# Expert gate/up tiles of 4 depth blocks by 1024 columns, activations transposed on VectorE, down rows in pairs

## What is computed

```python
def moe_ffn(u, router_w, w_gate_up, w_down):
    ...
    for e in range(N_EXPERTS):
        y = y + dense_gates[:, e:e + 1].astype(tok.dtype) * swiglu(tok, w_gate_up[e], w_down[e])
...
def swiglu(u, w_gate_up, w_down):
    g, up = jnp.split(u @ w_gate_up, 2, axis=-1)
    return (jax.nn.silu(g) * up) @ w_down
```

## Time and profile before

| | us |
|---|---|
| median of three runs | 1164.14 |
| span of the profiled execution | 1161.9 |
| first expert product in it | 423.45 |
| one job in it | 90.82 |
| TensorE busy | 1147.7 |
| VectorE busy | 289.3 |
| ScalarE busy | 284.7 |

### The profile page before, as it was taken

How to read it: one execution, slowest core, us unless ns; L and a number is a source line. 1 busy time by engine, 2 the same in 40 slices (tenths; PEclk the granted TensorE clock), 3 DMA queues, 4 the chain that set the end, 5 groups by cost and what they waited for, 6 DMA issues and landing times.

```text
span 1161.9 us, 31779 instructions
## 1 busy us (share of the span) xinstructions
PE 1147.7 (99%) x14480; PEld 1010.9 (87%) x14480; DVE 289.3 (25%) x474; ACT 284.7 (25%) x480; POOL 30.7 (3%) x84
## 2 busy tenths in 40 slices
PE   8999999999999999999999999999999999999997
PEld 7768999999998888888888888888888898988885
DVE  3776654554653430000000000000000000000002
ACT  4766543443548430011001011001001001001001
POOL 0000000000000011000000000000000000000100
PEclk9999999999999999999999999999999999999999
DMA  9649965552254399989999999999999999999993
GB/s 339 221 131 289 359 218 192 197 186 89 101 190 146 106 391 389 351 322 383 377 393 395 367 394 395 359 392 395 383 379 396 395 359 394 394 368 393 391 379 137
DMA packets 174368, 361.21 MB, mean 311 GB/s; under 512 B 6616, under 2 KB 50048, under 8 KB 174240
## 3 DMA queue, kind: packets, MB, share of 16 engines
q1 hardware_dynamic: 169936, 343.78, 80.7%
q0 software_dynamic: 4080, 15.34, 4.0%
q10 hardware_dynamic: 224, 0.09, 0.0%
HBM read 347.65 MB, written 11.53 MB: 309 GB/s over the span
## 4 chain that ended last, share of the span: by engine, by line
PE 92%; DMA 3%; DVE 2%; ACT 1%; SPq 1%; issue 0%; ACTq 0%; DVEq 0%
PE pair L962 57%; PE pair L531 9%; PE pair L532 9%; PE pair L533 9%; DMA dn_ring<-in_moe_w_down 3%; PE pair L1005 2%; PE pair L567 1%; PE pair L593 1%; SPq L462 1%; DMA norm_rows<-in_b_norm_w 0%; PE pair L944 0%; DVE up_lo L1626 0%; PE pair L632 0%; DVE dn_ring L1731 0%; PE pair L934 0%
## 5 line engine op out<-in xcount | busy, mean ns | idle before, releaser
L962 PE MATMUL pair<-up_ring,work 128*32 128x384 f32 (+1 forms) x6144 | 358.0, 380 | 0.0
L962 PEld LDWEIGHTS pair<-up_ring,work 128*32 128x32 f32 x6144 | 343.0, 110 | 9.5 <-issue 4.0
L962 PE MATMUL pair<-dn_ring,kT_a 128*32 128x256 f32 (+1 forms) x3168 | 250.5, 450 | 3.0 <-DMA dn_ring<-in_moe_w_down 2.1
L962 PEld LDWEIGHTS pair<-dn_ring,kT_a 128*32 128x32 f32 x3168 | 163.1, 110 | 61.5 <-DMA dn_ring<-in_moe_w_down 3.0
L2022 DVE TENSOR_TENSOR work<-work,pair 128x384 f32<-128x384 f32 x40 | 22.2, 554 | 507.0 <-PE pair L962 507.0
L1118 ACT ACTIVATE kT_a<-pair 128x384 f32<-128x384 f32 (+3 forms) x65 | 25.3, 401 | 488.6 <-PE pair L1005 488.5
L531 PE MATMUL pair<-uT_hi,up_hi 128*128 128x256 f32 x480 | 135.5, 282 | 0.8 <-DVE uT_lo L1640 0.6
L962 PE MATMUL pair<-up_more,work 128*32 128x384 f32 (+1 forms) x2304 | 136.0, 380 | 0.0
L532 PE MATMUL pair<-uT_lo,up_hi 128*128 128x256 f32 x480 | 134.8, 281 | 0.0
L533 PE MATMUL pair<-uT_hi,up_lo 128*128 128x256 f32 x480 | 134.8, 281 | 0.0
L1626 DVE TENSOR_TENSOR up_lo<-up_ring,up_hi 128x2048 fp32r<-128x2048 f32 x46 | 105.3, 2291 | 112.9 <-ACT up_hi L1118 112.8
(11 more groups left out here) (304 smaller groups left out, 794.8 us busy)
## 6 DMA issues: line engine op xcount, KB each, us to landing
up_ring<-in_moe_w_gate_up SPq DMA_DIRECT2D x128, 1024.0 KB, 13.0
dn_ring<-in_moe_w_down SPq DMA_DIRECT2D x88, 1024.0 KB, 15.1
up_more<-in_moe_w_gate_up SPq DMA_DIRECT2D x48, 1024.0 KB, 14.5
up_ring<-in_dense_w_gate_up SPq DMA_DIRECT2D x22, 1024.0 KB, 9.3
dn_ring<-in_dense_w_down SPq DMA_DIRECT2D x11, 1024.0 KB, 11.3
up_ring<-in_kv_w SPq DMA_DIRECT2D x4, 2048.0 KB, 8.1
y_rows<-q_T POOLq DMA_DIRECT2D x1, 6528.0 KB, 33.5
up_ring<-in_a_w_in SPq DMA_DIRECT2D x4, 1024.0 KB, 12.7
```

The costliest lines, as they stand in the source:

```text
L962: return pe.matmul(out, a, w, start=start, stop=stop, tile_position=(0, THIRD * place), skip_group_check=True)
```

## The change

- Gate and up tiles are 4 depth blocks by 1024 columns (768 in the last group). Four tiles make a group: gate with depth blocks 0 to 3 and 4 to 7, then up with the same. There are three groups, twelve tiles (E_UP). A row of a transfer is 4 KB (3 KB in the last group).
- In each depth block each third goes over all four places, 256 columns (192) a place, where place p takes columns 64p to 64p + 63 of every 256. PSUM holds the gate in one pair of banks and the up part in another (`gate_ps`, `up_ps`).
- The down weights are taken as rows 256m + 2p and 256m + 2p + 1 on partition p, so a partition's row of a transfer is 8 KB.
- Silu and product are made once for a group, and VectorE transposes the result in 32 x 32 blocks from `m_hid` to `m_hT`, both in memory of their own (`e_mem`, over `uT_hi` and `uT_lo`). `hidden_T` of TensorE and `hidden_step` of ScalarE go; VectorE's `hidden_step` is new.
- Down tile i - 4 follows up tile i (E_DN_LATE). SyncE issues down tile m behind up tile m + 6. Four down tiles are loaded ahead of the first job (one before), two of them in front of up tile 3.
- The slot-token product is made of six products on places instead of two on the whole array, an iteration earlier. The second saved result goes to slot T_MOE of `up_ring`.

```diff
-GROUPS = (STEPS + 1) // 2
+E_COLS = (1024, 1024, 768)
+GROUPS = len(E_COLS)
+E_UP = 4 * GROUPS
...
-        m_hid = work[:, 0:768].rearrange("p (b c) -> p b c", b=2)
+        m_hid = e_mem[:, 0:768]
...
-        m_hT = kT_a[:, :, :].rearrange("p h t -> p (h t)")[:, 0:3 * P].rearrange("p (f c) -> p f c", f=3)
+        m_hT = e_mem[:, 768:768 + GROUPS * 768].rearrange("p (g c) -> p g c", g=GROUPS)
...
-        tile_bank = (0, 1, 7)
+        gate_ps, up_ps = pair[0], pair[3]
...
-        DN_AFTER = 3
         FIRST = 3
         DN_LATE = 2
+        E_DN_LATE = 4
...
-            edn = moe_w_down[0].rearrange("e (b p) n -> e p b n", p=P)
+            edn = moe_w_down[0].rearrange("e (m p b) n -> e p m (b n)", p=P, b=2)

             def expert_up(i, e):
...
+                g, c0 = i // 4, sum(E_COLS[:i // 4])
+                for part in range(2):
+                    k = 4 * (i % 2) + 2 * part
+                    src = eup[bass.ds(e, 1), :, k:k + 2, i % 4 // 2, c0:c0 + E_COLS[g]]
+                    sp.dma_start(expert_cols(i)[:, 2 * part:2 * part + 2, :], src.rearrange("e p k c -> (e p) k c"))\
+                      .then_inc(expert_in(i), 16)
...
+                for i in range(E_RING, E_UP + E_RING):
+                    if i < E_UP or not last:
+                        sp.wait_ge(up_used, tile_done(i - E_RING, k))
+                        expert_up(i % E_UP, e if i < E_UP else next_e)
+                    m = i - E_RING
+                    if m < STEPS and not (first and m < RING):
+                        sp.wait_ge(dn_used, job_free(STEPS, m, k))
+                        expert_dn(m, e)
...
+            def expert_up(k, i):
...
+                if tile % 4 == 0 and i > 0:
+                    pe.wait_ge(e_silu, group_done(g - 1, job))
+                if tile % 4 == 2 and i > 2:
+                    pe.wait_ge(e_raw, group_done(g - 1, job))
+                ps, cols = (gate_ps, up_ps)[tile % 4 // 2], hidden_cols(g)
+                w = expert_cols(i).rearrange("p k (m c) -> p k m c", c=256)
+                for j in range(4):
+                    k_row = 4 * (tile % 2) + j
+                    for n in range(3):
+                        rows = m_u_now[:, SLOTS * k_row + THIRD * n:SLOTS * k_row + THIRD * n + THIRD]
+                        for place in range(4):
+                            out = part_of(ps, place)[:, 256 * n:256 * n + cols].rearrange("p (m c) -> p m c", c=64)
+                            mm = on_third(out, rows, w[:, j, :, 64 * place:64 * place + 64], place,
+                                          k_row == 0 and n != 1, k_row == KD - 1)
+                mm.then_inc(up_used, 1)
...
+            def silu_step(k, g, first=False):
+
+                act.wait_ge(up_used, tile_done(4 * g + 1, k))
+                if not first:
+                    act.wait_ge(e_hT, group_done(g - 1, k))
...
+            def hidden_step(k, g):
+                cols = hidden_cols(g)
+                dve.wait_ge(e_silu, group_done(g, k))
+                dve.wait_ge(up_used, tile_done(4 * g + 3, k))
+                v = m_hid[:, 0:3 * cols].rearrange("p (n c) -> p n c", n=3)
+                dve.tensor_tensor(v, v, up_ps[:, 0:768].rearrange("p (n c) -> p n c", n=3)[:, :, 0:cols], ALU.mult).then_inc(e_raw, 1)
+                dve.wait_ge(e_raw, group_done(g, k))
+                dve.transpose(m_hT[:, g, 0:3 * cols].rearrange("p (m b t) -> p m b t", b=2, t=THIRD),
+                              m_hid[:, 0:3 * cols].rearrange("p (m c b) -> p m b c", b=2, c=THIRD)).then_inc(e_hT, 1)
```

More of the change, by code:

```diff
@@ L94, in program @@
         u = sb("u", [P, NT, DM])
+        with nc.sbuf_tensor("e_mem", [P, 4096], f32) as e_mem:
+            pass
         uT_hi = sb("uT_hi", [P, KD, TOK], f32r)
@@ L278, in expert_slot @@
         def expert_slot(i):
-            return i % STEPS % E_RING
+            return i % E_UP % E_RING
         def expert_tile(i):
@@ L478, in _, with job @@
                 expert_up(i, 0)
-                expert_dn(i - DN_AFTER, 0)
-            def job(k, e, next_e, last=False):
-                for i in range(E_RING, STEPS + E_RING):
-                    if i < STEPS or not last:
-                        sp.wait_ge(up_used, job_up_free(i % STEPS, k + i // STEPS))
-                        expert_up(i % STEPS, e if i < STEPS else next_e)
-                    m = i - DN_AFTER
-                    if m < STEPS or not last:
-                        sp.wait_ge(dn_used, job_free(STEPS, m % STEPS, k + m // STEPS))
-                        expert_dn(m % STEPS, e if m < STEPS else next_e)
-            with sp.Fori(0, NEXP - 1) as k:
+            def job(k, e, next_e, first=False, last=False):
+                for i in range(E_RING, E_UP + E_RING):
[6 more added lines that the diff above has]
+                        expert_dn(m, e)
+            job(0, 0, 1, first=True)
+            with sp.Fori(1, NEXP - 1) as k:
                 job(k, k, k + 1)
@@ L1035, in right @@
                 def right(f):
-                    start, stop = i % STEPS == 0 and f == 0, i % STEPS == STEPS - 1 and f == 1
+                    start, stop = i == 0 and f == 0, i == STEPS - 1 and f == 1
                     for n in range(3):
@@ L1070, in iteration @@
                     mm.then_inc(e_pickT, 1)
-                if i >= DN_LATE and (i - DN_LATE < STEPS or not last):
-                    expert_dn(k, i - DN_LATE)
+                if 0 <= i - E_DN_LATE < STEPS:
+                    expert_dn(k, i - E_DN_LATE)
             def job(k, last=False):
-                for i in range(FIRST, STEPS + FIRST):
+                for i in range(FIRST, E_UP + FIRST):
                     iteration(k, i, last)
@@ L1471, in job @@
                 act.activation(one_out[:, :], ones[0:1, 0:1], ACT.Silu)
-                for i in range(FIRST, STEPS + FIRST):
+                for i in range(FIRST, E_UP + FIRST):
                     iteration(k, i, last)
-            for i in range(1, FIRST):
-                iteration(0, i)
+            silu_step(0, 0, first=True)
             with act.Fori(0, NEXP - 1) as k:
@@ L2035, in iteration @@
             def iteration(k, i, last=False):
-                g = hidden_group(i)
-                if g is not None and g != GROUPS - 1 and (g < GROUPS or not last):
-                    multiply_step(k, g)
-                if i == STEPS:
-                    multiply_step(k, GROUPS - 1)
-                if i == STEPS + 2:
+                if i % 4 == 3 and i < E_UP:
+                    hidden_step(k, i // 4)
+                if i == STEPS - 1 + E_DN_LATE:
                     result(k)
-                if i == 4 and not last:
+                if i == 3 and not last:
                     dve.wait_ge(e_gather, k + 1)
@@ L2051, in iteration @@
                     add_saved(y_in_first, y_first, 4, i - 7)
-                if last and i in (10, 11):
-                    add_saved(y_in_second, y_second, 5, i - 10)
+                if last and i in (9, 10):
+                    add_saved(y_in_second, y_second, 5, i - 9)
             def job(k, last=False):
-                for i in range(FIRST, STEPS + FIRST):
+                for i in range(FIRST, E_UP + FIRST):
                     iteration(k, i, last)
```

212 lines of the change are left out of this document (59 added, 153 removed).

## The result

The kernel after takes **1128.82 us** (median of four executions, 1127.64 to 1129.13), the kernel before 1163.46 beside it (1162.74 to 1164.34): a ratio of 0.9696, 95% interval 0.9683 to 0.971. That is 34.6 us less. The forecast was 1132, faster, in a range of 1118 to 1150. The profiled execution has a span of 1126.7 us.

What follows compares the result with a forecast made beforehand. TensorE was taken to bound the kernel, the DMA close behind: start 423.45 plus eight jobs of 87.0, 1.2 of waits, 8.7 of tail, 1 for meeting ends gave span 1130; 2.2 more made 1132 us, range 1118 to 1150.

Steps and rivals of the forecast that it cites:

- What bounds before: Expert stage of the kernel before: TensorE bounds at 90.82 us a job, the DMA needs 92.5 and lives on its lead.
- TensorE's job: TensorE's work for one expert: from 90.82 to 87.0 us, 3.85 us less a job, 30.8 over eight jobs.
- the loss of 4.0 ns a pass: TensorE's products: time lost per pass beside column streaming, drain at the transposes counted in, taken unchanged for the kernel after.
- The DMA's job: Transfers of one expert: longer rows at 406 GB/s bring 92.5 down to 89.6 us, bounds 88.0 and 92.0.
- the 4.4 us for result, gather and fetches: DMA time in a job beside the weights: 4.4 of 92.5 us before, kept unchanged for the kernel after.
- the sum 453.1 + 7.51 P: Span if the DMA sets the end, P being its us a job: 1126 for 89.6, 1144 for 92.0, 1114 for 88.0.
- rival (1): Expert weight transfers: longer rows bring up tiles little, TensorE waits in the last jobs; 92.0 us a job, 1146 us; chance 0.22.
- The last job's waits: TensorE in the last job: 1.2 of the 3.1 us of waits remain, since the transposes there go.
- the meeting of the two ends: Last two jobs: TensorE's end at 1129.3 and the DMA's at 1126 meet here and there, adding 1 us.
- no wait comes from the order while the lead lasts: SyncE's issue of down tiles: used 28.6 us after issue, where a landing takes 15.1, so no wait.
- VectorE's path: Product, transpose and signals before a group's first down tile: 2.1 to 4.5 us, covered by the next up tile, cost 0.
- Rival (2): TensorE's weight loads no faster than 53 ns each: 5.1 us a job more in the third group, 1172 us; chance 0.07.

Runs made afterwards that it cites:

- e1: Kernel before with the long-row transfers of the kernel after, products unchanged: 1161.26 us, 0.9981 of the kernel before.
- e5: Kernel after with gate/up rows of 2 and 1.5 KB and down tiles as two 512 KB transfers with 4 KB rows: 1160.65 us.
- e3: Kernel after with five groups of three 128x128 transposes a job put back on TensorE in the first seven jobs: 1148.49 us.
- e2: Kernel after with only the gate/up rows short (2 and 1.5 KB), down tiles as in the kernel after: 1155.61 us.
- e9: Kernel after with expert transfers in jobs 1 to 6 cut to a quarter of their bytes: 1125.86 us.
- e11: Kernel after with each down tile of the last job issued ahead of the gate/up tile beside it: 1126.93 us.
- e7: Kernel after with two spare VectorE products, some 4.6 us, ahead of each group's transpose: 1144.02 us.
- e6: Kernel after with the gate/up products halved on one place of four (place 3): 1157.27 us.
- e10: Kernel after with gate/up products halved on all four places and a quarter of the transfer bytes in jobs 1 to 6: 1215.33 us.
- e4: Kernel after with every gate/up product halved in columns on all four places, so twice the weight loads: 1372.94 us.
- e8: Kernel after with SyncE's branch turned round, so the last job's transfers stand right behind the test: 1130.12 us.

## Why the prediction was right

**What bounds before.** Right. e1 and e5 show the two bounds of the earlier trace rows from both sides: 2.2 us for the rows alone, 3.1 for TensorE's part alone. Had only one of the two been changed, this would have been a change of 0.2 to 0.3%.

**TensorE's job.** Forecast 86.97 us, measured 86.49. The mis-sized term is the loss of 4.0 ns a pass. The columns stream in 84.25 us (the prediction's 5.11, 3.83 and 2.55 us a tile); with the gather's 0.81 and the slot tokens' 0.31 off (the 0.31 is the prediction's, not measured apart), 1.1 us remain for 420 passes of a place, 2.7 ns each. The rest of the 4.0 was what the transposes did to the passes around them: e3's job has 0.15 us a group beside the 0.48 of the records, and 0.15 over the 120 passes between two groups are 1.3 ns. The prediction had named "the drain at the transposes" in the 4.0 and then kept it in the price of a pass when the transposes were gone. The gather went from 0.66 to 0.81 in the chain.

**The DMA's job.** Forecast 89.6 us, bounds 88.0 and 92.0. In the window from 523 it moved 406 GB/s while SyncE still waited for buffers, so 35.6 MB would take at most 87.7 us; in the window from 871, with fewer such waits, it moved 401, which is 88.8. So the job lies near the optimistic bound of 88.0, and the forecast's 89.6 was 1 to 2 us too much. Whether the rows of 8 KB gained more than the 2% that I allowed at best, or the 4.4 us for result, gather and fetches were too much, no run tells apart. By the Trainium skill ("DMA: Bandwidth & Descriptors", Why small descriptors are slow) the estimate was 90.4 us; the trace doesn't agree, it has 87.7 to 88.8, though the 4.4 us are in that estimate too. With these the sum 453.1 + 7.51 P gives 1112 to 1120: the DMA's end lies 7 to 15 us before TensorE's, not the 3 of the forecast.

**The price of rival (1).** e5 and e2 are this rival made real. At 382 GB/s a job of 35.6 MB takes 93.2 us and the sum gives 1153; the span was 1155.5. e2: at 384, 92.7 us, 1149 against 1153.1. So the sum is 2 to 4 us too low once the DMA is the bound, and the prediction's 1144 for up tiles without any gain from rows was too low by 9 (e2, which is that case) or 11.5 (e5): 5 and 9 of it because the rate is 384 and 382 over whole jobs and not the 387 that 92.0 us stand for.

**The last job's waits.** Forecast 1.2 of the 3.1 us, and 1 for the meeting of the two ends; measured 2.2 (1117.8 against 1115.6). That both terms together give the 2.2 is luck: e9 and e11 show that the waits are down tiles behind gate/up tiles in the queue, nothing to do with the transposes on which the 1.2 rested. What failed is the step "no wait comes from the order while the lead lasts", in both its numbers. It took a landing at 15.1 us from before; the last ones take 22. And it took 28.6 us from the issue to the use; the tile issued at 1065.55 was wanted at 1086.0, 20.4 us later, since it was issued some 8 us after its buffer was free. From 1028 to 1073 SyncE waits for buffers only 3.6 us, but a single issue takes it up to 5 us there, against less than 1 us in the window from 523.

**VectorE's path.** Forecast at no cost, with a path of 2.1 to 4.5 us: product, transpose and signals are 0.95 + 0.99 + 0.3 = 2.2 us, and the strided 32 x 32 transpose costs what a plain pass over 768 columns costs. e7 puts the cover between the two: with 4.6 us more, one group in three is late.

**The sum.** 423.7 + 691.9 + 2.2 + 8.9 = 1126.7; forecast 423.5 + 696 + 1.2 + 8.7 + 1 = 1130.4. Of the 3.7 us the jobs are 4.1 and the meeting 1, the waits -1 and the two ends -0.4.

**What it did not see.** How near the kernel is to a limit of its own instructions: in e6, 18% more passes cost 28.5 us. The prediction counted the passes of place 3, which were halved, but places 0 to 2 got more: in all 1490 records in 91 us before and 1581 in 87 after, 16.4 and 18.2 a us. Beside the full traffic the stops begin somewhere between 18 and 21 (means of windows; e6 has 20.8), and e10, at 110 GB/s, ran 29 a us and stood for 2 of 87 us. Rival (2) asked the right question, what many small products cost, and had the wrong mechanism.

## What to carry to other kernels

Where two resources stand within 2% of each other, cost both parts of a change together and each alone: 2 and 3 us here, and 35 together. Before counting on shorter products on TensorE's tiles, count its passes for each us of DMA traffic beside it; 18 passes a us ran without a stop here, 21 did not. In a queue that is 20 us deep the order of the issues decides what lands late, not when the issuing engine is free.

## What was unexpected of the hardware

- TensorE's stops of 0.6 to 3 us after 128 or 256 passes, from about 21 passes a us on, with 23 of 29 us a job at equal clock gone when the weight traffic falls to a quarter (e4, e6, e10).
- Four places side by side take a weight load every 29 ns, though one lasts 110 ns in the record (e4).
- The DMA engines moved 401 to 407 GB/s in windows of 87 us with rows of 3, 4 and 8 KB, and 381 to 384 with rows of 1.5, 2 and 4 KB once TensorE waited for them (e5).
- A branch of SyncE over unused code took it 5 us or more, and taking it away gained nothing (e8).
- After TensorE had stood for 3.6 us its granted clock was 0.50 (1.2 GHz) for about 5 us, which cost 2.8 us (e7).
- A 32 x 32 transpose of 128 x 768 values on VectorE takes 991 ns with strided reading, a product of the same size 954 ns.
